# Neighbourhood attention: turning the values once per token and fetching them from a scratch in device memory

## What is computed

```python
# 512 tokens = 8 grid rows x 64 columns; 16 heads of 64 channels
qkv = h @ w_qkv
# queries in 4 blocks of 16 columns; the keys of a block are all 8 rows x 32 columns
# the 32-column windows begin at columns 0, 8, 24, 32 and overlap
s = q_blk @ k_blk.T + bias            # 16 columns x 8 rows of queries, 256 keys
p = softmax(where(mask, s, -inf))
o = p @ v_blk                         # v_blk: the values of those 256 keys
return o @ w_out
```

## Time and profile before

| | |
|---|---|
| median of three runs | 2102.26 us |
| profiled execution | 2100.9 us, its span on the core 2099.1 us |
| PE busy | 2061.9 us, 98% of the span |
| DVE busy | 1237.2 us, 59% |
| ACT busy | 768.3 us, 37% |
| attention phase on PE | from about 399 us to 607 us |
| mean granted PE clock | 0.998 |
| DMA | 266.34 MB, mean 127 GB/s |

### The profile page before, as it was taken

How to read it: one execution, slowest core, us unless ns; L and a number is a source line. 1 busy time by engine, 2 the same in 40 slices (tenths; PEclk the granted TensorE clock), 3 DMA queues, 4 the chain that set the end, 5 groups by cost and what they waited for, 6 DMA issues and landing times.

```text
span 2099.1 us, 30437 instructions
## 1 busy us (share of the span) xinstructions
PE 2061.9 (98%) x10534; PEld 1701.5 (81%) x10534; DVE 1237.2 (59%) x1921; ACT 768.3 (37%) x1139; POOL 245.8 (12%) x238
## 2 busy tenths in 40 slices
PE   7999999999999999999999999999999999999997
PEld 6888888788888888888888888878888888888886
DVE  6867675656558667665635633477676664333344
ACT  5222222554444222223532222375656454322222
POOL 0000000431123000001300000141121240000002
PEclk9999999999999999999999999999999999999999
DMA  9767752233325667633335632332222123323322
GB/s 320 236 185 216 220 164 79 77 111 99 98 64 187 203 184 236 199 111 111 91 96 170 182 94 76 103 111 73 79 70 70 41 81 100 90 85 115 96 69 85
DMA packets 405669, 266.34 MB, mean 127 GB/s; under 512 B 9416, under 2 KB 366184, under 8 KB 405608
## 3 DMA queue, kind: packets, MB, share of 16 engines
q1 hardware_dynamic: 405608, 265.57, 42.0%
HBM read 263.37 MB, written 2.19 MB: 127 GB/s over the span
## 4 chain that ended last, share of the span: by engine, by line
PE 93%; DVE 3%; ACT 1%; POOL 1%; SPq 1%; issue 1%; DMA 0%; POOLq 0%; DVEq 0%; ACTq 0%
PE ps L1527 27%; PE ps L1529 27%; PE ps L1528 27%; PE ps L1578 1%; PE ps L1559 1%; PE ps L1815 1%; PE ps L1736 1%; PE ps L1762 1%; PE ps L1553 1%; PE ps L1747 1%; PE ps L1554 1%; PE ps L1833 1%; DVE x L1228 1%; PE ps L1570 1%; DVE w_lo L866 1%; PE ps L1572 1%
## 5 line engine op out<-in xcount | busy, mean ns | idle before, releaser
L866 DVE TENSOR_TENSOR w_lo<-raw,w_hi 128x1024 fp32r<-128x1024 f32 (+2 forms) x384 | 431.3, 1125 | 658.5 <-ACT w_hi L617 658.0
L617 ACT ACTIVATE w_hi<-raw 128x1024 fp32r<-128x1024 f32 (+2 forms) x384 | 371.8, 970 | 1091.4 <-PE ps L1529 1055.0
L1527 PE MATMUL ps<-h_hi,w_hi 128*128 128x512 f32 x1744 | 684.6, 393 | 1.9 <-ACT q_sig L696 1.4
L1529 PE MATMUL ps<-h_hi,w_lo 128*128 128x512 f32 x1744 | 679.3, 390 | 0.0
L1528 PE MATMUL ps<-h_lo,w_hi 128*128 128x512 f32 x1744 | 678.8, 389 | 0.0
L1527 PEld LDWEIGHTS ps<-h_hi,w_hi 128*128 128x128 f32 x1744 | 327.4, 188 | 73.4 <-issue 3.6
L1529 PEld LDWEIGHTS ps<-h_hi,w_lo 128*128 128x128 f32 x1744 | 327.4, 188 | 68.9
L1528 PEld LDWEIGHTS ps<-h_lo,w_hi 128*128 128x128 f32 x1744 | 327.6, 188 | 66.1
L1527 PE MATMUL ps<-g_hi,w_hi 128*128 128x512 f32 x704 | 274.8, 390 | 0.0
L1529 PE MATMUL ps<-g_hi,w_lo 128*128 128x512 f32 x704 | 274.0, 389 | 0.0
L1528 PE MATMUL ps<-g_lo,w_hi 128*128 128x512 f32 x704 | 273.9, 389 | 0.0
(11 more groups left out here) (262 smaller groups left out, 1930.6 us busy)
## 6 DMA issues: line engine op xcount, KB each, us to landing
raw<-in_ffn_w_in_dram SPq DMA_DIRECT2D x176, 512.0 KB, 3.7
ada_raw<-in_ada_w_dram SPq DMA_DIRECT2D x128, 512.0 KB, 4.1
raw<-in_ffn_w_out_dram SPq DMA_DIRECT2D x64, 384.0 KB, 3.5
raw<-in_ffn_w_out_dram SPq DMA_DIRECT2D x64, 320.0 KB, 3.1
raw<-in_hgrn_w_in_dram SPq DMA_DIRECT2D x40, 512.0 KB, 3.6
raw<-in_na_w_qkv_dram SPq DMA_DIRECT2D x24, 512.0 KB, 3.7
boot<-in_ada_w_dram SPq DMA_DIRECT2D x8, 512.0 KB, 7.4
boot<-in_ada_w_dram SPq DMA_DIRECT2D x16, 256.0 KB, 6.4
```

The source lines that it names most:

```text
L617: nc.scalar.activation(w_hi[s][:, 0:ph.kt, :], raw[s][:, 0:ph.kt, :], ACT.Copy).then_inc(S.w_hi_done, 1)
L866: nc.vector.tensor_tensor(w_lo[s][:, 0:ph.kt, :], raw[s][:, 0:ph.kt, :], w_hi[s][:, 0:ph.kt, :].bitcast(F32), ALU.subtract).then_inc(S.w_l ...
L1527: nc.tensor.matmul(ps[:, bank, :], w_hi[s][:, k, :], a, start=start and k == 0, stop=False)
L1529: ins = nc.tensor.matmul(ps[:, bank, :], w_lo[s][:, k, :], a, start=False, stop=stop and k == ph.kt - 1)
```

## The change

The values are copied once, as 128 channels x 512 tokens (`v_dim`), and turned once per token: four turnings of 128 x 128 into one PSUM bank. ACT copies that bank to `v_row` (tokens on partitions). SP stores `v_row` to a scratch `v_rows` in device memory, waits until the store has landed, and loads the eight windows of 128 keys from it into `v_key`, one DMA of 4 grid rows x 32 tokens x 512 bytes for each. `values` waits for these loads. SP's loop over the pairs is written out in full.

In the loop the store and the windows of pair i-2 stand behind the table loads of pair i. Those of pair 6 stand between the first and the second load of the output projection, those of pair 7 behind its fourth. The new tensors in SBUF have together the size of `v_win`.

```diff
+            def v_windows(j):
+                sp.wait_ge(S.vkey_ready, j + 1)
+                if not (isinstance(j, int) and j == 0):
+                    sp.wait_ge(S.vkey_in, j * (16 * CB * 2))
+                sp.dma_start(v_rows[:].rearrange("(b p) d -> p b d", p=P), v_row[:]).then_inc(S.v_stored, 16)
+                sp.wait_ge(S.v_stored, j * 16 + 16)
+                if not (isinstance(j, int) and j == 0):
+                    sp.wait_ge(S.pv_mm, j * 2)
+                for w in range(CB * 2):
+                    first = (w % 2) * (ROWS // 2) * GRID + KEY_START[w // 2]
+                    sp.dma_start(v_key[:, w], bass.AP(tensor=v_rows, offset=first * P,
+                                                      ap=[[GRID * P, ROWS // 2], [P, KW], [1, P]])).then_inc(S.vkey_in, 16)
...
-                with sp.Fori(1, ph.iters) as i:
...
+                if ph.kind == "na":
+                    for i in range(1, ph.iters):
+                        for s in range(ph.body):
+                            load(ph, i, s)
...
                         tab_loads(i)
+                        if i > 1:
+                            v_windows(i - 2)
...
                 for s in range(4):
                     if nxt is not None and s < nxt.body:
                         load(nxt, 0, s)
+                    if ph.kind == "na" and s == 0:
+                        v_windows(ph.iters - 2)
...
+                if ph.kind == "na":
+                    v_windows(ph.iters - 1)
...
-                        v = ps[:, 2 if isinstance(i, int) and i == 0 else 0, :].rearrange("p (r c) -> p r c", r=ROWS)
-                        for cb in range(CB):
-                            k0 = KEY_START[cb]
-                            ins = nc.scalar.activation(v_win[:, cb], v[:, :, k0:k0 + KW], ACT.Copy)
-                        ins.then_inc(S.v_ready, 1)
+                        nc.scalar.activation(v_dim[:], ps[:, 2 if isinstance(i, int) and i == 0 else 0, :], ACT.Copy).then_inc(S.v_ready, 1)
...
                 if not (isinstance(j, int) and j == 0):
-                    act.wait_ge(S.pv_mm, j * 2)
-                nc.scalar.activation(v_key[:], ps[:, 5:7, :], ACT.Copy).then_inc(S.vkey_ready, 1)
+                    act.wait_ge(S.v_stored, j * 16)
+                nc.scalar.activation(v_row[:], ps[:, 5, :], ACT.Copy).then_inc(S.vkey_ready, 1)
...
-                for w in range(CB * 2):
-                    src = v_win[:, w // 2].rearrange("p a b -> p (a b)")[:, (w % 2) * P:(w % 2 + 1) * P]
-                    ins = nc.tensor.transpose(ps[:, 5 + w // 4, (w % 4) * P:(w % 4 + 1) * P], src, ident[:])
+                for b in range(T // P):
+                    ins = nc.tensor.transpose(ps[:, 5, b * P:(b + 1) * P], v_dim[:, b * P:(b + 1) * P], ident[:])
...
                 pe.wait_ge(S.pt_ready1, i + 1)
+                pe.wait_ge(S.vkey_in, i * (16 * CB * 2) + 16 * CB * 2)
```

More of the change, by code:

```diff
@@ L171, in __init__ @@
         self.vkey_ready = sem("vkey_ready")
+        self.v_stored = sem("v_stored")
+        self.vkey_in = sem("vkey_in")
         self.s_mm = sem("s_mm")
@@ L340, in build @@
             k_sb = sb("k_sb", [P, ROWS, GRID], where=reg)
-            v_win = sb("v_win", [P, CB, ROWS, KW], where=reg)
+            v_dim = sb("v_dim", [P, T], where=reg)
+            v_row = sb("v_row", [P, T // P, P], where=reg)
             v_key = sb("v_key", [P, CB * 2, P], where=reg)
@@ L395, in build @@
         table = nc.dram_tensor("bias_rows", [NA_HEADS, RPB_R + 1, TAB_C], F32)
+        v_rows = nc.dram_tensor("v_rows", [T, P], F32)
         ps = ctx.enter_context(nc.psum_tensor("ps", [P, 8, 512], F32))
@@ L529, in tab_loads @@
                 for hp in range(2):
-                    if not isinstance(i, int):
+                    if i > 0:
                         sp.wait_ge(S.bias_done, i * 2 + hp - 1)
@@ L586, in _ @@
                     sp.wait_ge(S.g_ready, phases[n - 1].p0 + 2 * phases[n - 1].iters)
-                with sp.Fori(1, ph.iters) as i:
[L588 to L592, removed]
-                        tab_loads(i)
+                if ph.kind == "na":
+                    for i in range(1, ph.iters):
+                        for s in range(ph.body):
+                            load(ph, i, s)
+                            if ph.ada is not None:
+                                ada_loads(ph, i, s)
+                        tab_loads(i)
+                        if i > 1:
+                            v_windows(i - 2)
+                else:
+                    with sp.Fori(1, ph.iters) as i:
+                        for s in range(ph.body):
+                            load(ph, i, s)
+                            if ph.ada is not None:
+                                ada_loads(ph, i, s)
                 nxt = phases[n + 1] if n + 1 < len(phases) else None
```

## The result

The changed kernel takes 2108.08 us (median of nine runs, 2107.08 to 2109.49) against 2102.00 us for the kernel before in the same comparison. The ratio is 1.0031, with a 95% interval of 1.0022 to 1.0039: slower by 0.3%, or 6.1 us. The forecast was 2106.9 us, slower with a chance of 0.58, range 2101.5 to 2112.

The account below looks back on a forecast made before the run. PE was taken to bound the kernel (busy 2061.9 of 2099.1 us). Terms -4.0 + 0.4 + 6.2 + 2.0 = +4.6 us on 2102.26 gave 2106.9 us, range 2101.5 to 2112.

Parts of the forecast that it names:

- Turnings: PE, attention phase: four of eight turnings go in each of eight steps, 0.43 us each, 3.4 us saved.
- First scores: PE's wait for ACT's four `v_win` copies at the first scores ends 0.6 us earlier, and that is kept.
- Added waits on PE: A fifth wait ahead of `values` on PE, 0.09 us each, 0.7 for eight at most; taken as +0.4 us.
- Covers inside the loop: Next pair's weight load and window data land 7 and 5 us before they are needed; cost zero.
- The stall: End of phase: second output-projection load, behind pair 6's windows on SP, delays PE's last turning 6.2 us (3.4 to 8.9).
- The clock: After the roughly 6 us PE stall, the following work runs at a lower clock: +2.0 us, ends 0 and 3.
- The end of the phase: Last `values`: pair 7's windows land at 598.9 against a start at 600.1, covered by 1.2 us.
- Writing out SP's loop: Unrolling SP's loop adds instructions on a queue that has time; cost zero.
- windows on four engines: Window loads run on four DMA engines, not sixteen: stall 8.1 us, net +6.8, 2109.1 us; chance 0.25.
- the sum by the table rows: The prediction's own sum, window issues priced at 0.62 us each from table loads: +4.6 us, 2106.9 us; chance 0.45.
- rival 3: End of phase: the late weight load is hidden and stops nobody, so the kernel gains, 2098.7 us; chance 0.07.
- rival 4: Windows come late in every pair, some 3 us in each of six, more at the end: about +40, 2142 us; chance 0.05.

Follow-up runs that it names:

- e7: Kernel before with one value copy and four turnings, no scratch, ACT copying one bank twice (wrong values); 3.9 us less than before, ratio 0.9979.
- second profile: From the changed kernel run once more, unedited, in a later comparison; median 6.0 us over the kernel before, ratio 1.0032.
- e4: Changed kernel with each window load reading 128 tokens in a row instead of 4 rows of 32 (wrong values); 3.0 us over before, ratio 1.0013.
- e5: Changed kernel with 26 unread identity products on PE in its idle time before pair 7's last turning; 4.4 us over before, ratio 1.0021.
- e6: Kernel before with only SP's loop over the pairs written out in full; 0.3 us less than before, ratio 0.9997, interval including 1.
- e1: Changed kernel with pair 6's store and windows moved behind all four output-projection loads on SP; 2098.6 us against 2101.38 before, ratio 0.9987.
- e8: Kernel before with one SP wait holding the second output-projection load until pair 7's first turning is done; 5.7 us over before, ratio 1.0024.

## Why the prediction held, and where it was off

- **Turnings, -3.4.** 0.46 us a pair in place of 0.43; right. e7 shows the gain by itself.
- **First scores, -0.6.** PE's wait went from 1.4 to 0.8, right for that wait. I looked only one step further, at `k_sb`. The first pair's probabilities are late too, as their bias is made late on POOL, and PE waits 0.5 for them. This term I put at nothing. e7, with no scratch, has the same 0.5.
- **Added waits on PE, +0.4.** Nothing to be seen: the pair got shorter by as much as the turnings give. It should have been zero.
- **Covers inside the loop.** Right for the pairs after the first, wrong for the first. There the store landed after 6.5 us, and I had allowed 2.6 and some 3 more for the table loads ahead of it; PE waited 0.9 in one profile, 0.8 in the other.
- **The stall, 6.2.** The step that was mis-sized: it is 7.8 (7.4 in the second profile). The path is the one forecast. The store cost less than I took (2.2 against 2.6), the eight issues 5.4 against 5.0. The miss is the landing of the weight load, 577.99 - 572.79 = 5.2 us and not 3.7. I had priced the windows by the table loads' issues and let the weight load find the DMA engines free. It did not: the windows flow at 87 GB/s, 0.75 us for each 64 KB, slower than SP issues them at first, so four engines were still behind. In e4, without that, the landing is 4.3 and the wait 5.2. That the issues came near is luck: in e4 eight take 3.7; here five go out in 2.8 us (567.38 to 570.17) and the last three take 2.6, with the backlog that I left out. The low end of the range has a slip: 567.5 + 2.0 + 3.0 + 3.7 is 576.2, not 576.0.
- **The clock, +2.0.** 3.1 and 2.0 in two profiles, of which some 0.2, as in e5, is not the clock's; the size was right within what it varies.
- **The end of the phase.** I called it covered by 1.2 us; PE waited 0.2 there in one profile and not in the other. From the store to the last landing it is 608.37 - 596.78 = 11.6 us, where I had 10.0, again the windows' flow.
- **Writing out SP's loop, zero.** e6: zero.

Of the rivals, the first (windows on four engines, 2109.1 us) names the right mechanism for the windows, and the measured 2108.1 lies between its time and mine. That my 2106.9 is so near is in part luck: in the first profile the parts sum to +8.2 against my +4.6, as the stall is 1.6 longer, the clock's part 1.1, and the small waits of 1.1 and 0.5 were not in the sum; the median moved by less than either profile. I gave the four engines 0.25 against 0.45 for the sum by the table rows, which have sixteen rows in their outer step; those rows were near in kind, but not in the outermost step, which e4 shows to decide. Hiding (rival 3) was excluded by SP's order, and e1 shows that it needed only that order to be another. Nothing was late in every pair (rival 4).

What stays open: the medians are 6.1 and 6.0 us over before, the two profiled phases 8.6 and 6.8. Between the two profiles 1.1 us is the clock's part and 0.4 the long wait. How these parts are spread over the timed runs is not seen.

## What to carry to other kernels

A new wait on a queue must be priced by what stands behind it at every place where it is put. The last pass of a pipelined loop is such a place: the other engines took up the next phase's work in another order there, so a load that had landed some 15 us before it was wanted (issued at 553.4, some 3.7 to land, taken at 572.3) became the one that PE waited for. Moving the wait behind loads that need only their slot, and nothing of the scratch, made 8.9 us of difference (from +6.1 to -2.8 against before). And where a kernel is bound by PE, price an idle stretch with the clock behind it: the four here, 4.0 to 7.8 us long, cost 1.8 to 3.1 us more, between a quarter and a little over half of the wait itself.

## What the runs showed of the hardware that was not expected

- A DMA whose source has an outermost step of 4 (4 x 32 rows of 512 B) moved at 82 to 97 GB/s against up to 347 for the weight loads. The same bytes as one step of 128 rows reached 277 (e4). Behind such loads the next DMA of the queue pays too: a 512 KB load landed after 5.2 us, against 4.3 in e4 and a median of 3.7 before.
- Issues on SP took longer for these windows, 5.4 us for eight against 3.7 in e4, and the later ones more than the first: five in 2.8 us, then three in 2.6. That the later ones wait for the engines that are behind is the fitting reason; it is not shown by itself.
- After an idle stretch of PE as short as 4.0 us (e8) its next rows ran partly at the lower clock, 0.58 granted in 584 to 586: 1.8 us lost on 7.1 us of work.
